# A two-block transformer kernel: squares and splits at the start put in another order, and the norm of the gated heads beside the transform along tokens

## What is computed

```python
def rms_norm(x, gain=None):
    y = x * rsqrt(mean(x * x, axis=-1) + EPS)
    return y if gain is None else y * gain
def modulate(h, shift, scale):
    return h * (1.0 + scale) + shift

for l in range(DEPTH):
    mx = split(silu(c) @ w_mod[l] + b_mod[l], N_MOD)        # 9 vectors of 1024, for x
    mz = split(silu(c_ctx) @ w_mod[l] + b_mod[l], N_MOD)    # the same for ctx
    x = x + 0.5 * mx[2] * swiglu(modulate(rms_norm(x), mx[0], mx[1]), w1, w3, w2)
    z = z + 0.5 * mz[2] * swiglu(modulate(rms_norm(z), mz[0], mz[1]), w1, w3, w2)
    hx, hz = modulate(rms_norm(x), mx[3], mx[4]) @ w_in[l], modulate(rms_norm(z), mz[3], mz[4]) @ w_in[l]
    # mixing: fft2 over tokens and features | neighborhood attention | gated linear attention | attention
    mix_x = concat(a_x, b_x, rms_norm(gla_x, gla_norm) * silu(gla_r), d_x)
    x = x + mx[5] * (mix_x @ w_out[l])
    ...                                                      # a second swiglu, then the second stack
```

## Time and profile before

| | before |
|---|---|
| median of 3 runs | 2461.11 us (2460.64 to 2464.52) |
| the profiled execution's own time | 2459.61 us |
| its span, first to last instruction | 2457.5 us |
| PE busy (matmul) | 2389.6 us, 97% |
| DVE / ACT / POOL busy | 1511.0 / 1004.7 / 395.5 us |
| mean granted TensorE clock | 0.997 |
| DMA | 362.50 MB, mean 148 GB/s |

### The profile page before, as it was taken

The page is one execution under the profiler, slowest core; times in us unless marked ns, Lnnn a source line. Parts: engine busy times, 40 slices in busy tenths (PEclk is TensorE's granted clock), DMA queues, the critical chain, the costliest instruction groups (busy, mean ns, idle before and its releaser), DMA issues.

```text
span 2457.5 us, 39377 instructions
## 1 busy us (share of the span) xinstructions
PE 2389.6 (97%) x15054; PEld 2098.7 (85%) x15054; DVE 1511.0 (61%) x2554; ACT 1004.7 (41%) x1659; POOL 395.5 (16%) x403
## 2 busy tenths in 40 slices
PE   6999999999999999999999999999999999999998
PEld 4888888677888888888888877999988999989998
DVE  5878765683699865523323575665666665666664
ACT  5222224554522223432223454545445444446443
POOL 2221211240122131111011131121000120000220
PEclk9999999999999999999999999999999999999999
DMA  8556542112366764222332222555533555434554
GB/s 318 199 195 212 181 163 82 65 52 78 99 217 230 246 222 163 86 95 95 96 101 95 86 69 80 170 182 182 162 104 129 173 176 176 146 113 144 190 189 138
DMA packets 97881, 362.50 MB, mean 148 GB/s; under 512 B 11024, under 2 KB 11280, under 8 KB 96560
## 3 DMA queue, kind: packets, MB, share of 16 engines
q1 hardware_dynamic: 75744, 274.42, 34.0%
q0 software_dynamic: 21968, 85.72, 10.2%
HBM read 359.04 MB, written 1.05 MB: 147 GB/s over the span
## 4 chain that ended last, share of the span: by engine, by line
PE 87%; DVE 4%; ACT 4%; issue 2%; DMA 1%; POOL 0%; ACTq 0%; DVEq 0%; SPq 0%; POOLq 0%
PE bank L741 27%; PE bank L743 26%; PE bank L742 26%; ACT ring_high L1230 2%; DVE ring_low L1695 1%; PE bank L1017 1%; PE bank L1005 1%; PE bank L987 1%; PE bank L1039 1%; DMA ring<-stream_dram 0%; PE bank L958 0%; PE bank L966 0%; DVE arena L1761 0%; PE bank L1180 0%; PE bank L1095 0%
## 5 line engine op out<-in xcount | busy, mean ns | idle before, releaser
L1695 DVE TENSOR_TENSOR ring_low<-ring,ring_high 128x1024 fp32r<-128x1024 f32 x524 | 647.0, 1235 | 559.4 <-ACT ring_high L1230 557.5
L741 PE MATMUL bank<-x_parts,ring_high 128*128 128x512 f32 (+2 forms) x2700 | 912.6, 338 | 14.6 <-DVE ring_low L1695 11.2
L743 PE MATMUL bank<-x_parts,ring_low 128*128 128x512 f32 (+2 forms) x2700 | 900.3, 333 | 0.0
L742 PE MATMUL bank<-x_parts,ring_high 128*128 128x512 f32 (+2 forms) x2700 | 898.9, 333 | 0.0
L1230 ACT ACTIVATE ring_high<-ring 128x1024 fp32r<-128x1024 f32 x524 | 551.5, 1054 | 630.1 <-PE bank L743 627.5
L741 PEld LDWEIGHTS bank<-x_parts,ring_high 128*128 128x128 f32 x2700 | 510.2, 189 | 79.7 <-issue 19.2
L743 PEld LDWEIGHTS bank<-x_parts,ring_low 128*128 128x128 f32 x2700 | 510.2, 189 | 48.3
L742 PEld LDWEIGHTS bank<-x_parts,ring_high 128*128 128x128 f32 x2700 | 510.3, 189 | 47.2 <-issue 0.2
L604 POOL TENSOR_TENSOR hidden_parts<-fresh,hidden_parts 128x512 fp32r<-128x512 f32 (+2 forms) x132 | 215.3, 1631 | 1359.9 <-ACT hidden_parts L1345 1359.9
L741 PE MATMUL bank<-hidden_parts,ring_high 128*128 128x512 f32 (+2 forms) x1122 | 368.2, 328 | 0.3 <-POOL hidden_parts L604 0.3
L743 PE MATMUL bank<-hidden_parts,ring_low 128*128 128x512 f32 (+2 forms) x1122 | 367.4, 327 | 0.0
(11 more groups left out here) (226 smaller groups left out, 2163.5 us busy)
## 6 DMA issues: line engine op xcount, KB each, us to landing
ring<-stream_dram SPq DMA_DIRECT2D x521, 512.0 KB, 3.4
mod_ring<-w_mod_dram POOLq DMA_DIRECT2D x128, 512.0 KB, 5.1
arena<-w_mod_first_dram POOLq DMA_DIRECT2D x8, 1024.0 KB, 11.6
ring<-stream_dram POOLq DMA_DIRECT2D x3, 512.0 KB, 13.1
arena<-na_bias_dram POOLq DMA_DIRECT2D x2, 768.0 KB, 11.4
mod_ring<-consts_dram POOLq DMA_DIRECT2D x1, 1140.0 KB, 5.4
resid<-x_dram POOLq DMA_DIRECT2D x2, 512.0 KB, 6.3
resid<-ctx_dram POOLq DMA_DIRECT2D x2, 512.0 KB, 9.6
```

Source lines behind the costliest of these rows:

```text
L741: pe.matmul(out, w[0][:, b], xh, start=start, stop=False)
L742: pe.matmul(out, w[0][:, b], xl, start=False, stop=False)
L743: return pe.matmul(out, w[1][:, b], xh, start=False, stop=stop)
L1695: dve.tensor_tensor(low[:, u % RING], ring[:, u % RING], high_f[:, u % RING], ALU.subtract).then_inc(low_parts, 1)
```

## The change

At the start:

- POOL issues x, then ctx, then `w_mod_first[0]`, units 0 and 1, `w_mod_first[1]`, `[2]`, unit 2 and the rest.
- ACT squares four chunks per operation (four operations of 128 x 4 x 256 in place of 16 of 128 x 256) into `scaled`; DVE halves them in three additions per stream (4, 2, 1 chunks wide) in place of seven.
- Both means go to one bank, and one inverse root of 512 columns takes the place of two of 256. The first mean stands ahead of modulation 0, the second behind turn 0.
- PE makes `part(0, c - 1)` and `part(1, c - 1)` from c = 1, `part(2, c - 3)` from c = 3; five parts are left for the end in place of eight.
- ACT and DVE split unit 2 behind chunk 1, and ACT splits unit 3 right behind chunk 7, ahead of the first Silu of the feed-forward. Silu of `c` and `c_ctx` moves into step 1 of `ffn`; the dot products of steps 0 and 1 are both made in step 1 (`c_turn`).

At the end of the mixing: the two `head_mean` stand behind `dft_tokens` of x; ACT squares the gated heads ahead of its copies of the transform. In layer 0 ACT's inverse roots and DVE's scaling and gating (`gla_finish`) stand ahead of the part for ctx; in layer 1 they stay behind.

```diff
@@ after()
-                return list(range(KC)), both, META, ("ffn1", 0), (0, 0)
+                return [], both, META, ("ffn1", 0), (0, 0)
@@ POOL
+            for i in range(2):
+                pool.dma_start(resid[:, i * half:(i + 1) * half, META:META + NX], A["x"][...]).then_inc(...)
+            for i in range(2):
+                pool.dma_start(resid[:, i * half:(i + 1) * half, META + NX:META + N1], A["ctx"][...]).then_inc(...)
             for c in range(KC):
...
                 pool.dma_start(first_mod[:, c % FIRST_SLOTS], ...)
+                for s in ((0, 1), (), (2,))[c] if c < 3 else ():
+                    pool.dma_start(ring[:, s], A["stream"][s]).then_inc(...)
@@ PE, start_units
+                means = take("mean", ("start",))
+                pe.wait_ge(*when("consts_loaded", 0))
+                pe.wait_ge(*when("first_sums", 0))
+                pe.matmul(means[:, 0:NX], cst(C_ONESD), sumsq[:, 0:NX], start=True, stop=True)
                 pe.wait_ge(*when("c_cols_silu", 0))
-                for c in range(KC):
+                first_modulation(0)
+                first_turn(0)
+                pe.wait_ge(*when("first_sums", 1))
+                pe.matmul(means[:, NX:N1], cst(C_ONESD), sumsq[:, NX:N1], start=True, stop=True).then_inc(...)
+                for c in range(1, KC):
                     first_modulation(c)
...
-                    if c >= 4:
-                        part(2, c - 4)
+                    if c >= 3:
+                        part(2, c - 3)
                     first_turn(c)
-                    if c >= 2:
-                        part(0, c - 2)
-                        part(1, c - 2)
+                    part(0, c - 1)
+                    part(1, c - 1)
                 pe.wait_ge(*when("consts_loaded_rest", 0))
-                for i, c in ((0, 6), (1, 6), (2, 4), (2, 5), (0, 7), (1, 7), (2, 6), (2, 7)):
+                for i, c in ((2, 5), (0, 7), (1, 7), (2, 6), (2, 7)):
                     part(i, c)
@@ PE, mixing
                         for s in range(2 - l):
                             dft_tokens(l, s)
-                for i in range(2):
-                    head_mean(("gla", l), i, N1 if l == 0 else NX)
+                            if s == 0:
+                                for i in range(2):
+                                    head_mean(("gla", l), i, n)
@@ ACT, ffn
+                if tag == ("ffn1", 0):
+                    split_ahead(1)
...
-                            if tag == ("ffn2", 0) and h == 0 and f == 0:
+                            if tag in (("ffn1", 0), ("ffn2", 0)) and h == 0 and f == c_turn(tag):
...
-                            split_ahead(1)
+                            if tag != ("ffn1", 0) or h or f:
+                                split_ahead(1)
@@ ACT, mixing, step len(PROJ1) + 1
+                        for i in range(2):
+                            head_square(("gla", l), i, when("gla_out_sb", l, 1 - l, i), proj1[:, GLAQ + i, 0:n], n)
                         for s in range(2 - l):
+                            if s == 1:
+                                for i in range(2):
+                                    head_root(("gla", l), i, n)
                             act.wait_ge(*when("dft_l", l, s))
@@ ACT, the start
             for g in range(2):
-                for d in range(KC):
-                    square(("start",), d, g, ...)
-                first_rows(g)
-                if g == 1:
-                    split_ahead(1 - RING)
-                root_of_mean(("start",), g)
+                a, b = norm_cols(("start",), g)
+                for i in range(2):
+                    act.wait_ge(*when(f"ctx_loaded{i}" if g else f"x_loaded{i}", i))
+                    c = slice(i * half, (i + 1) * half)
+                    act.activation(scaled[:, c, a:b], resid[:, c, META + a:META + b], ACT.Square).then_inc(...)
+            first_rows(0)
+            split_ahead(1 - RING)
+            act.wait_ge(*when("mean", ("start",)))
+            inverse_root(rstd[:, 0], bank("mean", ("start",)), N1, ("start",), ("mean", ("start",)))
             first_high(0)
             split_ahead(1)
-            first_high(1)
-            first_rows(2)
-            split_ahead(1)
-            first_high(2)
-            for c in range(3, KC):
+            for c in range(1, KC):
                 first_rows(c)
                 first_high(c)
-            for s in range(2):
-                act.activation(csilu[:, s], csilu[:, s], ACT.Silu).then_inc(*made("c_silu", 0, s))
+                if c == 1:
+                    split_ahead(1)
@@ DVE, ffn (todo: the dot products of this step)
+                    if l is not None and h == 0 and g <= c_turn(tag):
+                        todo = list(itertools.chain(*(mod_chunks(l, h, i) for i in range(g + 1)))) if g == c_turn(tag) else []
@@ DVE, mixing, step len(PROJ1) + 1; gla_finish holds what stood behind mixing(l), and is called there for l == 1
                         for s in range(2 - l):
+                            if s == 1:
+                                gla_finish(l)
@@ DVE, the start
             for g in range(2):
-                for d in range(KC):
-                    sum_squares(("start",), d, g)
-                if g == 0:
-                    dve.wait_ge(*when("small_loaded", 0))
-                first_shift_scale(g)
+                a, b = norm_cols(("start",), g)
+                dve.wait_ge(*when("first_squares", g, 1))
+                dve.tensor_tensor(scaled[:, 0:4, a:b], scaled[:, 0:4, a:b], scaled[:, 4:8, a:b], ALU.add).then_inc(...)
...
+                dve.tensor_tensor(scaled[:, 0:2, a:b], scaled[:, 0:2, a:b], scaled[:, 2:4, a:b], ALU.add).then_inc(...)
...
+                dve.tensor_tensor(sumsq[:, a:b], scaled[:, 0, a:b], scaled[:, 1, a:b], ALU.add).then_inc(...)
+            dve.wait_ge(*when("small_loaded", 0))
+            first_shift_scale(0)
```

71 lines of the change are left out of this document (39 added, 32 removed).

## The result

| | before | after |
|---|---|---|
| median, same chip | 2462.82 us (6 runs, 2460.64 to 2465.12) | 2454.12 us (6 runs, 2452.91 to 2455.55) |
| ratio | | 0.9971, 95% interval 0.9961 to 0.9981 |
| the profiled execution's own time, its span | 2459.61, 2457.5 us | 2455.15, 2452.6 us |
| PE / DVE / ACT busy | 2389.6 / 1511.0 / 1004.7 us | 2391.4 / 1510.6 / 1002.6 us |

The change made the kernel 0.29% faster by the ratio; the two medians alone would give 0.35%. The six times of before fall in two groups of three, 2460.64 to 2461.11 and 2464.52 to 2465.12, and their median lies between the groups, so the 8.7 us between the medians is a little flattering: in a later set of runs (`after_again`) it is 7.2. The forecast of 2455.2 us is 1.1 above the median and the range holds it.

A forecast was written before the change was run, and what follows sets the result against it. PE's own work was taken as the bound, so gains come from gaps: start 3.9 plus mixing 2.0 is 5.9 us off 2459.61, giving 2453.7; with 1.5 up to the median, 2455.2 us, range 2452.6 to 2459.3.

The forecast's parts named there:

- The start: From the first loads to PE's first matmul with unit 3: ends at 54.4 instead of 58.26, 3.9 us earlier.
- x is complete at about 8.8: First step of the start's load timeline: x landed by 8.8 us, then ctx at 11.4 and modulation 0's weights at 14.0.
- What was moved and hidden: Silu and two dot products moved into feed-forward step 1: costed at nothing, 0.4 us without cover.
- The mixing: Waits for squares of the gated heads go: 1.00 us in layer 0, 0.99 in layer 1, together 2.0 us.
- What is late next: Layer 0's mixing: projection chunks 0 and 1 wait for ctx, ready by 597.4, asked for at 601.2.
- Whatever the start ends earlier should reach the end of the program whole: After the start: PE has no long gap before the mixing's seam, so the start's gain carries through undiminished.
- The clock at the start: When TensorE's clock rises in the start: assumed high at 29.15; 2.2 us more gain if early, 2.7 less if late.
- the unknown of size: The moment TensorE's clock rises in the start, which no profile row decides: 2.2 us more gain to 2.7 less.
- Its middle: The assumed case for the start's clock: high at 29.15, as long after turn 1 as before after turn 2.
- the late end: Start: clock held low until the end of part (2,0), 2.7 us less gain, total 2457.9; chance 0.22.
- The slower rival: Whole program: clock falls in gaps where it held, 3.0 us each, four make 12.0, total 2467.2; chance 0.04.

The follow-up runs named there:

- after_again: The changed kernel run once more, unaltered, beside the variants: median 2454.12 us, ratio 0.9971 to the kernel before.
- start_only: The changed kernel with its mixing part taken back, so only the start is changed: median 2457.97 us, ratio 0.9985 to the kernel before.
- mix_only: The kernel before with only the mixing part of the change: median 2459.94 us, ratio 0.9994 to the kernel before.
- squares_only: The kernel before with the wide squares, three additions and one root, everything else in the old order: median 2459.83 us, ratio 0.9996.
- held_gaps: The changed kernel with small matmuls of constants ahead of five waits, one of them misplaced: median 2454.98 us, ratio 0.9971 to before.
- held_all: The changed kernel with modulation 1's rows copied earlier, filler matmuls through the start and ahead of five mid-program waits: 2447.25 us, ratio 0.9942 to before.

## Why the prediction was right, step by step

- **The start** was forecast at 3.9 us and is 4.55 (53.71) and 4.11 (54.15) in two profiles. The order of events is as written: weights of modulation 0 later by 2.2 (13.59, forecast 14.0), first scaled chunk 19.59 (20.15), turn 1 22.43 (23.1), turn 2 28.48 (29.15), modulation 3 30.50 (31.15), chunks 3.73 apart (3.72), a new wait of 0.41 (0.5), unit 3 53.71 (54.4). Most of the difference stems from the first step: "x is complete at about 8.8". ACT starts on the first half of x at 6.80, on its second at 8.08, and 0.4 of the 0.65 was there when modulation 0 began; 0.2 more came by the logarithm (18.13, forecast 18.75), for turn 0 and the mean behind it took 2.1 us where I had 2.25, and the turn came 0.44 behind its rows where I had 0.50. The 2.6 us for 1 MB held (10.97 for the second half of ctx, 13.59 for the weights). The Trainium skill, "DMA: Bandwidth & Descriptors", Anatomy of one DMA, by which the weights were to land at 13.6 (an estimate from its figure), met 13.59, but by two errors: the same late end of x, and 2.4 us for 1 MB where this trace has 2.6.
- **What the parts are worth** I had not split. Taken one at a time: Silu and unit 3 1.9, the squares 1.4, the loads 0.3; the order of the parts would have the rest of the 4.1, if they may be added; it has no run of its own.
- **What was moved and hidden** cost nothing, as costed: PE has no wait over 0.06 us from the first matmul with unit 3 to 200 us.
- **The mixing** was forecast at 2.0 us: 1.00 and 0.99. It is 1.1 in layer 0 and 1.2 in layer 1. "What is late next" held: nothing took the place of the squares.
- **"Whatever the start ends earlier should reach the end of the program whole"** was the weak sentence. Its reason was misread, to begin with: I wrote that PE has no long gap between the first feed-forward step and the seam, but the kernel before waits 1.83 us there (to 458.42); it did no harm in the change's profile, where the lead is 4.5 on both sides of it. By the path alone the change is worth 7.9, of which 0.8 is a wait of 0.53 at 1555 and what hangs on it, which only the profile of before has, and 0.2 is in small differences of other waits. 0 to 2.7 us are lost near 777 by profile, and 3.0 more go to the clock in the change's.
- **The clock at the start** was the unknown of size. Its middle came in both profiles of the change; the late end came in `start_only`, 3.3 where I had 2.7.
- **The slower rival** (the clock falls in gaps where it held) was right as a mechanism, wrong in its terms. I priced a fall at 3.0 and knew of one. There are two to five before the end, counted as 1.7 or 3.4 us each, and those that the waits allow to be read cost 1.5 and 3.1. Of the profiles without fillers in the mixing, those with the new start and an early clock lost 8.5 or 10.2, and the others (before, `mix_only`, `squares_only`, `start_only`) 5.1 or 6.8. So the change's profile has 3.0 us more of them (3.4 as counted), not four times 3.0, and they are the reason that a path shorter by 7.9 gave 4.9 in the profiled execution. That the shift itself brings them was not tested; one profile for each kernel is little.
- **That the total came out within 1.1 us** is luck in part, for three errors of mixed sign are in it. The path was under-sized by 2.0 (7.9 against 5.9), and the clock took 3.0 of which none was in the sum: the profiled execution should have been at 2453.7 and was at 2455.15. The third is the step from it to the median: I added 1.5 us, because the profile of before lay that much below its median, but the change's lies 1.0 above its own. So 1.45 too low became 1.1 too high.

## What to carry to other kernels

Where PE bounds a kernel and the trace shows gaps of one to four microseconds, list the granted clock behind each gap before pricing an edit: what a gap costs is its length plus what the clock loses behind it. Matmuls without effect, placed exactly where PE waits and no longer than the wait, bought about as much here (6.9 us, one moved copy included) as the whole re-ordering (7.2 to 8.7); misplaced by one step they cost their full length. Do not add up time at the low clock as if all of it were lost: price a stretch by how far two traces drift apart over it. And follow an edit's lead through the trace at waits that both profiles share: a lead can be given back 200 us later, to an engine that was never near the edit.

## What the runs showed that I had not expected

- In the profile of before the granted clock reads 1.00 over the whole start, though matmuls of 512 columns start 0.43 us apart there; in `mix_only`, the same start, it reads 0.50 from 17.8 to 34.9. In the start the distance of matmuls is to be believed, not the column.
- The clock fell behind waits of 1.53 to 2.17 us (1757, 1778, 2120, 454) in some profiles and held in others at the same place; behind the waits of 1.64 us near 663 and 1.53 near 1558 it never fell in fourteen profiles. Which wait is hit is open. That work in the wait keeps the clock is shown by the four places together: the twelve profiles without fillers there have 30 stretches in 48 chances, at least one each, and `held_gaps` and `held_all` have none in 8. At one place alone it is not shown, for other profiles had none there either.
- Matmuls of zeros count as work: 22 of them raised the clock at 5 us.
- POOL's subtraction of 128 x 512 took 1.46 or 2.24 us, and a small operation of DVE 0.18 or 1.15, by what ran on the other engine (`mix_only`). That this is a shared path to memory was not tested.
